# A transformer layer on one core: down-projection reloads moved to GpSimd's queue, residual kept in the output, and layer-norm channel tiles summed on VectorE

## The reference, cut to what matters

```python
proj = modulate(rms_norm(x, norm_mix_w), sh1, sc1) @ w_in
attn_out = windowed_gqa_with_context(q, k, v, k_ctx, v_ctx, sink)   # 8 heads of 64, +-128 tokens and the context
u = ga * sigmoid(gb)                                  # 512 channels
u = depthwise_conv(u, conv_w, conv_b)                 # 31 taps
u = silu(layer_norm(u, conv_norm_w, conv_norm_b))     # over the 512 channels
x = x + g1 * (concat([attn_out, u]) @ w_out)
h2 = modulate(rms_norm(x, norm_ffn_w), sh2, sc2)
gate, val = split(depthwise_conv(h2 @ w_up, ...))     # 2 x 2816 columns, 3 taps
x = x + g2 * ((silu(gate) * val) @ w_down)
```

## Time and profile before

| | |
|---|---|
| median of three executions | 1235.33 us (1234.78 to 1236.83) |
| the profiled execution's own time | 1237.15 us |
| its span, first to last instruction | 1235.3 us |
| mean granted TensorE clock | 0.964 of 2.4 GHz |
| TensorE, VectorE, ScalarE, GpSimd busy | 94%, 77%, 47%, 26% |

### The profile page before, as it was taken

How to read it: one execution, slowest core, us unless ns; L and a number is a source line. 1 busy time by engine, 2 the same in 40 slices (tenths; PEclk the granted TensorE clock), 3 DMA queues, 4 the chain that set the end, 5 groups by cost and what they waited for, 6 DMA issues and landing times.

```text
span 1235.3 us, 16863 instructions
## 1 busy us (share of the span) xinstructions
PE 1159.9 (94%) x5837; PEld 962.4 (78%) x5837; DVE 948.4 (77%) x1403; ACT 580.2 (47%) x993; POOL 315.4 (26%) x335
## 2 busy tenths in 40 slices
PE   5799999889999999998799999999999998999997
PEld 1378888788888987786588888788788876888885
DVE  0479988679984454458999999999999967788687
ACT  4452356765545563545443444434444434444441
POOL 2100011134563000000544453635520000002256
PEclk9899999989899879999899999999999998999998
DMA  9322555519999013222445445355342285335352
GB/s 376 109 73 71 130 103 114 143 33 258 266 261 273 2 53 110 105 76 69 154 130 176 152 136 170 120 169 158 131 153 78 76 320 200 103 104 159 102 162 85
DMA packets 102833, 174.90 MB, mean 142 GB/s; under 512 B 9322, under 2 KB 62690, under 8 KB 101748
## 3 DMA queue, kind: packets, MB, share of 16 engines
q1 hardware_dynamic: 84692, 112.04, 27.1%
q0 software_dynamic: 16928, 57.88, 18.9%
q10 hardware_dynamic: 1152, 4.19, 0.9%
HBM read 116.41 MB, written 30.41 MB: 119 GB/s over the span
## 4 chain that ended last, share of the span: by engine, by line
PE 36%; DVE 12%; issue 5%; ACT 4%; DMA 3%; POOL 1%; DVEq 0%; ACTq 0%; SPq 0%; POOLq 0%
PE ps L1527 16%; PE ps L1492 5%; PE ps L1577 5%; PE ps L1578 5%; PE ps L1579 5%; DVE y L1931 2%; DVE w_op L1830 2%; DMA hid<-hid_scratch 2%; DVE w_raw L1848 1%; DVE y L1927 1%; ACT y L1722 1%; ACT w_op L1642 1%; POOL p_all L2099 1%; DVE u L1920 1%; DVE s_sum L1848 1%
## 5 line engine op out<-in xcount | busy, mean ns | idle before, releaser
L1527 PE MATMUL ps<-t_op,w_op 128*128 128x512 f32 x1056 | 247.3, 390 | 2.8 <-issue 0.9
L1527 PEld LDWEIGHTS ps<-t_op,w_op 128*128 128x128 f32 x1056 | 197.7, 188 | 46.3 <-issue 3.2
L1527 PE MATMUL ps<-hx,w_op 128*128 128x512 f32 x792 | 191.8, 396 | 10.1 <-DVE u L1920 6.9
L1527 PEld LDWEIGHTS ps<-hx,w_op 128*128 128x128 f32 x792 | 150.8, 191 | 44.0 <-DVE u L1920 6.5
L1642 ACT ACTIVATE w_op<-w_raw 128x512 fp32r<-128x512 f32 x132 | 80.0, 623 | 196.8 <-DVE w_raw L1848 186.9
L1577 PE MATMUL ps<-dnh,ah 128*128 128x512 f32 x308 | 121.8, 395 | 10.5 <-DVE dnl L1938 10.5
L1578 PE MATMUL ps<-dnl,ah 128*128 128x512 f32 x308 | 121.0, 393 | 0.0
L1579 PE MATMUL ps<-dnh,al 128*128 128x512 f32 x308 | 120.8, 392 | 0.0
L1830 DVE TENSOR_TENSOR w_op<-w_raw,w_op 128x512 fp32r<-128x512 f32 x132 | 101.8, 785 | 10.0 <-ACT w_op L1642 7.7
L1742 ACT ACTIVATE ah<-hid 128x512 fp32r<-128x512 f32 x77 | 48.7, 632 | 112.8 <-PE ps L1579 104.3
L2076 POOL DMA_DIRECT2D wd<-in_w_down x44 | 32.0, 729 | 270.5 <-DVE h_first L1819 193.4
(11 more groups left out here) (288 smaller groups left out, 2411.7 us busy)
## 6 DMA issues: line engine op xcount, KB each, us to landing
w_raw<-in_w_up SPq DMA_DIRECT2D x44, 512.0 KB, 5.2
wm<-in_w_mod SPq DMA_DIRECT2D x32, 512.0 KB, 6.0
sums<-wm POOLq DMA_DIRECT2D x32, 512.0 KB, 7.9
wd<-in_w_down POOLq DMA_DIRECT2D x44, 256.0 KB, 3.3
w_down_sums<-wd POOLq DMA_DIRECT2D x44, 256.0 KB, 2.8
dn_raw<-w_down_sums SPq DMA_DIRECT2D x44, 256.0 KB, 2.7
hid_scratch<-hid SPq DMA_DIRECT2D x20, 512.0 KB, 4.4
hid<-hid_scratch SPq DMA_DIRECT2D x20, 512.0 KB, 5.3
```

Of the source, the lines that this page charges most:

```text
L1527: last = pe.matmul(bank_of(p, s), w_op[p][w][:, k, :], rows_of(p, k, v), start=(start and k == 0 and w == 0 and v == 0), stop=(k == KH - 1 ...
```

## The change

Attention and layer norm: taps and joins are spread over groups 1 to 9 and `LN` goes from 9 to 10. VectorE adds the four channel tiles (`channel_sums`) before the means and the four tiles of squares (`square_total`) before the variance, so TensorE handles one tile in each. The variance moves into PSUM columns of its own and the middle of group 12. Column and row sums both stand behind the loop, with the last turn-over between them. The silus stand in the next block, on ScalarE ahead of the operand copies. Two operand tiles of w_out trade places in memory, with the waits that belong to this.

Down-projection: the order is (1, 2, 6, 5, 7, 3, 4). The reloads are in GpSimd's list, in another order, the first two a hidden tile earlier. SP's list holds only the weight loads. x1 is stored straight into the output. VectorE does all gate multiplications (`quad`, which has the former `read_quad` and four new kinds), and GpSimd adds the results into the output by accumulating DMAs. Product 2 adds to product 1's banks, which ScalarE copies one by one as they finish. Waits that count steps follow the new order.

The diff, cut to its core:

```diff
-        TAP_GRP = 5
+        TAP_GRP = (0, 4, 4, 4, 4, 4, 5, 5, 5, 5)
...
-        JOIN_AT = ((), (3,), (3,), (3,), (3,), (3,), (3,), (1, 3), (1, 3))
+        JOIN_AT = ((), (3,), (3,), (3,), (3,), (3,), (3,), (3,), (3,), (1, 2))
...
+        MOD_BANK = 4 + first_item[NGRP] % 2
+        LN = 10
...
-                    if n == LN:
-                        pe.wait_ge(tap_done, NTAP)
-                        pe.wait_ge(join_done, JOINS)
                     if n in (LN, LN + 1):
-                        for ct in range(CTL):
-                            last = pe.matmul(ps[:, 7, :], meanw[:], cacc[:, ct, half(n - LN)], start=(ct == 0), stop=(ct == CTL - 1))
-                        last.then_inc(ln_mm, 1)
-                    elif n == LN + 2:
-                        pe.wait_ge(ln_act, 2 * CTL)
-                        for b in range(TT):
-                            for ct in range(CTL):
-                                last = pe.matmul(ps[:, 7, b:b + 1], sqc[ct][:, b * P:(b + 1) * P], meanw[:, 0:1], start=(ct == 0), stop=(ct == CTL - 1))
-                        last.then_inc(ln_mm, 1)
+                        pe.wait_ge(ln_sum, 3)
+                        pe.matmul(ps[:, 7, :], meanw[:], sqc[0][:, half(n - LN)], start=True, stop=True).then_inc(ln_mm, 1)
...
+                def variance():
+                    pe.wait_ge(ln_dve, 8)
+                    pe.wait_ge(o_lo, LN + 1)
+                    pe.wait_ge(ln_sum, 9)
+                    for b in range(TT):
+                        last = pe.matmul(ps[:, 7, VAR_COL + b:VAR_COL + b + 1], sqc[0][:, b * P:(b + 1) * P], meanw[:, 0:1], start=True, stop=True)
+                    last.then_inc(ln_mm, 1)
+
+                def column_sums(c):
+                    pe.wait_ge(mod_acc[1 + c], 16 * KT)
+                    for j in range(KT):
+                        o = c * KT + j
+                        last = pe.matmul(ps[:, MOD_BANK, o:o + 1], sums[1 + c][:, j * P:(j + 1) * P], ones[:, 0:1], start=True, stop=True)
+                    last.then_inc(col_mm, 1)
+
+                def row_sums(r):
+                    pe.wait_ge(mod_acc[3 * r], 16 * KT)
+                    for hh in range(2):
+                        pe.matmul(ps[:, 2 * r + hh, :], ones[:], sums[3 * r][:, half(hh)], start=True, stop=True).then_inc(row_mm, 1)
...
-                for r in range(2):
-                    pe.wait_ge(mod_acc[3 * r], 16 * KT)
-                    for hh in range(2):
-                        pe.matmul(ps[:, 2 * r + hh, :], ones[:], sums[3 * r][:, half(hh)], start=True, stop=True).then_inc(row_mm, 1)
+                column_sums(0)
+                row_sums(0)
+                column_sums(1)
                 turn_outputs(NGRP - 1)
+                row_sums(1)
...
-                        if n == NGRP - 1 and j < CTL:
-                            act.wait_ge(ln_dve, 19)
-                            act.activation(cacc[:, j, :], cacc[:, j, :], ACT.Silu, scale=cols[:, C_CNW + j:C_CNW + j + 1],
-                                           bias=cols[:, C_CNB + j:C_CNB + j + 1]).then_inc(silu5, 1)
...
+                def summed(dst, a, b, n):
+                    dve.wait_ge(ln_sum, n - 1) if n > 1 else None
+                    dve.tensor_tensor(out=dst, in0=a, in1=b, op=ALU.add).then_inc(ln_sum, 1)
...
+                def channel_sums(i):
+                    if i == 0:
+                        dve.wait_ge(tap_done, NTAP)
+                        dve.wait_ge(join_done, JOINS)
+                        summed(sqc[0][:], cacc[:, 0, :], cacc[:, 1, :], 1)
+                    elif i == 1:
+                        summed(sqc[1][:], cacc[:, 2, :], cacc[:, 3, :], 2)
+                    else:
+                        summed(sqc[0][:], sqc[0][:], sqc[1][:], 3)
+
+                def square_total(hh, i):
+                    dve.wait_ge(ln_act, CTL * (hh + 1))
+                    h, n = half(hh), 4 + 3 * hh + i
+                    a, b = ((0, 1), (2, 3), (0, 2))[i]
+                    summed(sqc[a][:, h], sqc[a][:, h], sqc[b][:, h], n)
...
+                        if n == LN - 1 and j in (3, 4):
+                            channel_sums(j - 3)
+                        elif n == LN and j == 0:
+                            channel_sums(2)
+                        elif n == LN + 1 and j in (3, 4):
+                            square_total(0, j - 3)
+                        elif n == LN + 2 and j == 0:
+                            square_total(0, 2)
+                            square_total(1, 0)
+                        elif n == LN + 2 and j == 1:
+                            square_total(1, 1)
+                            square_total(1, 2)
+                        elif n == LN + 2 and j == 2:
+                            variance_read()
...
-        DOWN = (1, 6, 2, 5, 7, 3, 4)
+        DOWN = (1, 2, 6, 5, 7, 3, 4)
         NSTEP = len(DOWN) * NK2
-        UPPER = (1, 2, 7, 4)
-        POOL_STEPS = 28
+        UPPER = (1, 2, 5, 3)
+        QUAD_OPS = [("c11", t) for t in range(4)] + [("u2", t) for t in range(4)] + [("u4", t) for t in range(4)]
+        QUAD_OPS += [(name, t) for t in range(4) for name in ("s22", "c22", "w21")]
+        QUAD_OPS += [(name, t) for t in range(4) for name in ("s12", "c12")] + [("c21", t) for t in range(4)]
+        SIX_BEHIND = 6
...
-            RELOADS = (3, 2, 21, 20, 5, 4, 7, 6, 9, 8, 11, 10, 13, 12, 15, 14, 17, 16, 19, 18)
+            RELOADS = (21, 20, 3, 2, 5, 7, 9, 11, 13, 15, 4, 6, 8, 10, 17, 19, 12, 14, 16, 18)
...
-                    sp.dma_start(x1_dram[t * P:(t + 1) * P, :], xt[:, t % NXT, :]).then_inc(x1_out, 16)
+                    sp.dma_start(out[0, t * P:(t + 1) * P, :], xt[:, t % NXT, :]).then_inc(x1_out, 16)
...
-                sp.wait_ge(up_lo, split_at(4, FT - 1))
-                for s in range(2):
-                    sp.wait_ge(hid_out[s], 8 * RING)
-                for i in range(16):
-                    reload(i)
-                for i in range(16, 20):
-                    load_step(i - 12)
-                    reload(i)
-                for n in range(8, NSTEP):
+                for n in range(4, NSTEP):
                     load_step(n)
-                for t in range(TT // 2):
-                    sp.wait_ge(quad_read, 20 + 2 * t + 2)
-                    sp.dma_start(out[0, (TT // 2 + t) * P:(TT // 2 + t + 1) * P, 0:HALF], gout[1][:, t, :]).then_inc(last_stored, 16)
-                sp.wait_ge(last_stored, 16 * (TT // 2))
...
+                        if n == NK2:
+                            pe.wait_ge(p1_copied, t + 1)
                         last = down_product(n, t)
+                        if n == NK2 - 1 and t < TT // 2 - 1:
+                            last.then_inc(bank_mm, 1)
...
+                act.wait_ge(ln_dve, 19)
                 for ct in range(CTL):
+                    act.activation(cacc[:, ct, :], cacc[:, ct, :], ACT.Silu, scale=cols[:, C_CNW + ct:C_CNW + ct + 1],
+                                   bias=cols[:, C_CNB + ct:C_CNB + ct + 1]).then_inc(silu5, 1)
+                    act.wait_ge(silu5, ct + 1)
...
+                            if t < TT // 2 - 1:
+                                act.wait_ge(bank_mm, t + 1)
+                            else:
+                                act.wait_ge(dn_mm, NK2)
...
+                    elif name == "c22":
+                        ins = dve.tensor_tensor(out=g22[:, t, :], in0=u4_all[:, t, :], in1=g2[1], op=ALU.mult)
+                    elif name == "w21":
+                        ins = dve.tensor_tensor(out=w21[:, t, :], in0=u2_all[:, t, :], in1=g2[0], op=ALU.mult)
...
+                    if p == 6 and i < SIX_BEHIND:
+                        down_sum(6, NK2 - SIX_BEHIND + i)
                     down_low(n)
-                    if p == 1:
-                        down_sum(5, i - 3)
-                        if i == NK2 - 1:
-                            for last_i in range(NK2 - 3, NK2):
-                                down_sum(5, last_i)
-                    elif p == 2:
-                        down_sum(3, i)
+                    if p == 2:
+                        down_sum(5, i)
+                        if i >= SIX_BEHIND:
+                            down_sum(6, i - SIX_BEHIND)
                     elif p == 5:
                         down_sum(7, i)
-                    before = {2: 6, 5: 2, 7: 5, 3: 7, 4: 3}.get(p)
-                    if before and i in (1, 3, 5, 7):
-                        read_quad(before, i // 2)
+                    elif p == 7:
+                        down_sum(3, i)
+                    if i in (1, 3, 5, 7):
+                        for name in {6: ("c11",), 5: ("u2",), 7: ("u4",), 3: ("s22", "c22", "w21"), 4: ("s12", "c12")}.get(p, ()):
+                            quad(name, i // 2)
...
-                    dve.wait_ge(bank_mm, t + 1)
...
+                    quad("c21", t)
...
-                def step(out, a, b, op):
-                    if steps[0]:
-                        pool.wait_ge(pool_step, steps[0])
```

(31 more changed lines are left out.)

163 lines of the change are left out of this document (57 added, 106 removed).

## The result

The changed kernel takes 1216.8 us (median of 4 runs, 1213.7 to 1225.0) beside 1235.05 us for the kernel before (4 runs, 1232.95 to 1236.8): a ratio of 0.986, with a 95% interval from 0.983 to 0.990. Ratios leave out runs that are over 1.5% above the fastest of the same kernel. It is faster, by 18.2 us where 35 were forecast, and 1216.8 lies above the range.

What follows compares the result with a forecast made beforehand. TensorE, occupied for 94% of the span, was taken as the bound. Attention and layer norm minus 22.6 and down-projection minus 13.2, together minus 35.8, took 1237.15 to 1201.4; 1199.5 for the median, rounded to 1200 us, range 1191 to 1213.

Steps and rivals of the forecast that it cites:

- The end of the span: From TensorE's last product to the span's end, 5.65 us before: minus 1.2 us, between minus 2.3 and plus 0.2.
- One-column products at full clock: Group 12's 16 variance products at 0.09 us, plus 2.5; modulation sums behind the loop plus 2.5, net minus 5.0.
- the clock falls again: Attention rival: group 12 loses 3.6 us more, work behind the loop 4, w_out's start 2; about 1210; chance 0.2.
- Group 11: Attention: loses all its one-column variance products and the half clock, 12.4 us like group 13; minus 12.0.
- group 9: Attention: gets 5 taps, 2 joins, 2 adds, loses 3.60 us on TensorE; 16.0 us, 0.6 more than before.
- group 13: Attention: trades its normalising multiplies for the diagonal of group 12; minus 0.8 us.
- taps and joins: Attention groups 1 to 8: moving some to group 9 saves 2.7 us for taps and 2.2 for joins.
- Group 10: Attention: keeps 2 of 8 wide products for the means, taking 12.6 us; minus 3.0.
- Down stage: Down-projection, step 0 to last product: minus 12.0 us, from the waits before step 4 and at the end going.
- The silus: On ScalarE ahead of the w_out operands: cost 0 with 2.8 us to spare; up to 6.3 without cover.
- The wait before step 4 is for its weights: Down-projection: SyncE issues 16 reloads before that load; moving them saves 5.35 us and 1.7 of slow clock.
- step 4 stays late because the weights are slow from traffic: Down-projection rival, also covering GpSimd's reloads lagging: the wait stays, keeping 7 us, 1207; chance 0.1.

Runs made afterwards that it cites:

- the kernel with the plain last quarter: Changed kernel with the last output quarter's residual added by VectorE and stored plainly by SyncE, eight accumulates fewer: 1209.3 us, ratio 0.979.
- the longer trace above: Trace of the changed kernel with SyncE in place of GpSimd waiting for the last accumulating store to land: 1211.8 us.
- the experiment: The kernel with the plain last quarter, with taps and joins put back in groups 1 to 8: 1209.8 us.
- its plain stores: Changed kernel with its 20 accumulating stores made plain on GpSimd's queue, leaving the output incomplete: 1216.6 us, ratio 0.988.

## Why the prediction was wrong

Two of its terms were mis-sized, and one of its bounds was drawn from the wrong rows. Either miss alone would have left the time inside 1191 to 1213: by the tables above, 1207 with the miss at the end and 1211 with that of the attention (estimates; the kernel with the plain last quarter, which keeps only the second, measured 1209.3).

**The end of the span** is the step that failed outright: "I take 3.1, the plain store of this size from GpSimd, and 0.4 behind: minus 1.2 (minus 2.3 to plus 0.2)". It measured +6.3. The last landing was 5.5 (5.0 in the median of four) and not 3.1, above the upper bound of 4.5: an accumulate of twice the size into SBUF was no upper bound for one into DRAM. Multiply and queue took 1.5 and not 1.0. The largest miss is "0.4 behind", which was SyncE's: 5.1 us lie behind GpSimd's last landing, 4.6 of them its `DRAIN`. The rows for a GpSimd store gave its landing, but all 12 of those stores were issued before 1215, and SyncE's list ended last. The trace of the kernel before does have that `DRAIN`, 4.95 us long, hidden under SyncE's last stores; the forecast does not count it.

**One-column products at full clock.** "At 0.09 us, the pace of the first ones, 1.5" for group 12, and the alternation behind the loop at "plus 2.5, so minus 5.0 together". Group 12 measured +6.4 in place of +2.5, the stretch behind the loop +2.6 in place of -5.0: 11.5 us in all, by the table. The rival "the clock falls again" is what happened, with the places it named; it had 0.2 and a price of 9.6 us. Put on the forecast of 1199.5 that price gives 1209, and the end's 7.5 give 1216.6, beside 1216.8 measured; that they meet so closely is luck, since the stages of the traces above differ by more. An estimate from the granted clock points the same way: group 12 has a mean of 0.78 over 17.4 us and the stretch behind the loop 0.68 over 19.2, which is 3.9 and 6.1 us lost. That the one-column products themselves bring the clock down is not shown. Groups 9 and 10 have none and fell to 0.89 and 0.91 on average, and with the variance behind other work its 16 products took 1.92 us, the full-clock pace. The argument against it, that the stretches were shorter with wide products between, was wrong: in the longer trace above the wide products ran at half clock as well.

By the Trainium skill ("TensorE: Matmul & The Clock Gate", Part 1: The HAM clock gate) the clock follows how busy TensorE has been. The fall behind an idle stretch agrees with that. That the clock then stayed down does not: 4.00 us busy of 4.00 at 0.50, and so from 432 to 454.

**Terms that held.** Group 11 (-11.7 for -12.0), group 9 (+0.7 for +0.6 in the mean, 15.5 to 17.7 us), group 13 and, within 1.3, taps and joins. Group 10 gave half of its 3.0. Down stage: -12.6 for -12.0, the splits and both waits as described. The silus cost nothing.

**Right size, wrong cause.** "The wait before step 4 is for its weights: SP issues 16 reloads" had the right wait and took its place in the list for the reason. The two loads of x1 made 3.7 of its 5.2 us; the forecast mentions in passing that they fall away. The rival "step 4 stays late because the weights are slow from traffic" had the cause, and missed that the change removes the traffic too. The total came out right because both went.

**Taps and joins** gave their gain and lost it in group 9, as two terms that cancel once group 9 is bound by VectorE: in the experiment +5.3 and -5.0. The forecast counted 4.9 against 0.6, since in its trace of before group 9 took 15.4 us with no tap in it; the old group 9 lost that time to TensorE's wide products, which the three sums replaced. Where the products go, the taps' place is free to choose.

**The trace of before** was long in groups 1 to 8: 104.5 us, where three other traces of the same code show 97.3 to 97.4. The sum was made against it. This moved no term, but a gain read from that pair alone (18.3 up to w_out) is 7 us above the 11.0 that the means of four and five traces give.

## What to carry to other kernels

A DMA's price at the end of a kernel is not its landing time in the middle: here 5 us followed the last landing when GpSimd's list ended last, and 0.4 when SyncE's did. Look at what each engine does at the very end of its list, in the trace of before too. Accumulate into the output where work still follows, and let the last quarter leave by plain stores from SyncE. Price narrow products at the lower clock unless a trace shows them at the upper one with the same neighbours, and look for TensorE's waits just before them; filling one came with 5 us. Read more than one trace of the kernel before, where a stage has waits that depend on how DMA and GpSimd fall in time.

## What was not expected of the hardware

- GpSimd's list closes with a `DRAIN` of 4.1 to 5.8 us. When it comes last, the span ends 5.1 us behind the last landing (changed kernel), 6.2 (its plain stores) or 4.7 (kernel before with its last stores moved). It is 3.1 with SyncE waiting beside it, and 0.4 when both stores and wait are SyncE's.
- An accumulate of 256 KB into DRAM lands after 3.6 to 7.3 us, 4.2 in the median, and plain stores in its place take 2.3 at the end. Of two issued back to back the second took 6.7 in the median.
- The same instructions behind the loop took 15.0 and 24.4 us in the traces of two kernels that don't differ there; in the longer the granted clock was 0.50 from 432 to 454 us, with TensorE occupied all the while.
- 2.1 MB of loads beside 16 reloads of 512 KB lengthened those from 23.6 to 26.5 us, and TensorE's wait for the load behind them from 1.5 to 5.2.
